# A hybrid decoder layer: the depthwise convolution wholly on VectorE, and the counting of a threshold search divided anew between ScalarE and VectorE

## The reference, cut to what matters

```python
s = einsum('thd,ld->thl', qi, ki) * 64 ** -0.5               # indexer
score = einsum('th,thl->tl', wi * 8 ** -0.5, relu(s))        # causal, -inf above the diagonal
_, idx = top_k(score, 256)                                   # 256 keys per query
attn = softmax(q . k[idx] + rel_bias) . v[idx]               # 8 heads x 64
u = glu_a * sigmoid(glu_b)                                   # 512 channels
conv = silu(layer_norm(depthwise_causal_conv(u, dw_w) + dw_b))   # 31 taps
y = x + concat(attn * silu(gate_a), conv * silu(gate_c)) @ w_out
```

## Time and profile before

| | us |
|---|---|
| runs | 1110.79, 1114.1, 1116.92 |
| the profiled execution | 1112.72 |
| its span | 1110.9 |
| PE busy | 965.8 (87%) |
| DVE busy | 762.6 (69%) |
| ACT busy | 388.1 (35%) |
| POOL busy | 178.4 (16%) |
| PE, DVE in the chain that ended last | 52%, 36% |

### The profile page before, as it was taken

The page is one execution under the profiler, slowest core; times in us unless marked ns, Lnnn a source line. Parts: engine busy times, 40 slices in busy tenths (PEclk is TensorE's granted clock), DMA queues, the critical chain, the costliest instruction groups (busy, mean ns, idle before and its releaser), DMA issues.

```text
span 1110.9 us, 11534 instructions
## 1 busy us (share of the span) xinstructions
PE 965.8 (87%) x3902; PEld 517.6 (47%) x3902; DVE 762.6 (69%) x1770; ACT 388.1 (35%) x808; POOL 178.4 (16%) x120
## 2 busy tenths in 40 slices
PE   3999999096899999999978999792899788899998
PEld 3866666063233444666433334441443433464443
DVE  5207979999897877999998889956777643552000
ACT  6311343141566545555510000216442432462000
POOL 0200699370342000000000000001013012000000
PEclk9899999588999999999998889896898997999999
DMA  7450020020472212020002000005024112100222
GB/s 276 149 183 0 1 76 2 0 77 0 152 231 81 105 38 96 1 76 1 1 9 104 20 19 11 1 0 198 21 84 116 30 39 57 29 2 12 76 76 66
DMA packets 35355, 69.89 MB, mean 63 GB/s; under 512 B 9633, under 2 KB 11977, under 8 KB 35289
## 3 DMA queue, kind: packets, MB, share of 16 engines
q1 hardware_dynamic: 28129, 43.99, 11.6%
q0 software_dynamic: 7168, 25.17, 7.1%
HBM read 58.50 MB, written 11.12 MB: 63 GB/s over the span
## 4 chain that ended last, share of the span: by engine, by line
PE 52%; DVE 36%; ACT 4%; issue 4%; DMA 2%; POOL 2%; SPq 0%; DVEq 0%; ACTq 0%; POOLq 0%
PE ps L485 48%; DVE ctmp L1297 11%; PE ps L488 4%; DVE junk L1363 4%; DVE eqm L1363 4%; POOL ctmp L1796 2%; DVE ct L1275 1%; ACT PTs L926 1%; DMA KVr<-in_cache_v,idx 1%; DVE Pm L1742 1%; DVE pv L1499 1%; DMA xn<-in_x_prompt 1%; DVE ps L1737 1%; DVE LG L1626 1%; DVE prod L1624 1%
## 5 line engine op out<-in xcount | busy, mean ns | idle before, releaser
L485 PE MATMUL ps<-xT,W 128*128 128x344 f32 x960 | 286.6, 461 | 1.8 <-ACT gcT L926 1.8
L485 PEld LDWEIGHTS ps<-xT,W 128*128 128x128 f32 x960 | 184.9, 194 | 101.5 <-issue 7.4
L485 PE MATMUL ps<-W,xT 128*128 128x512 f32 (+3 forms) x576 | 216.3, 534 | 2.0 <-ACT relu L1086 1.2
L1297 DVE SCALAR_TENSOR_TENSOR ctmp<-uT,chw,ctmp 128x1024 f32<-128x1024 f32 x90 | 172.4, 1916 | 3.1
L485 PEld LDWEIGHTS ps<-W,xT 128*128 128x128 f32 (+1 forms) x576 | 95.8, 187 | 115.3 <-issue 115.1
L1118 ACT ACTIVATE sgj<-SC,candn 128x1024 bf16<-128x1024 f32 (+2 forms) x96 | 88.6, 924 | 49.7 <-DVE candn L1379 49.7
L1796 POOL TENSOR_TENSOR ctmp<-ctmp,product 128x1024 f32<-128x1024 f32 x30 | 91.7, 3057 | 29.3 <-ACT product L1014 26.3
L1836 POOL DMA_INDIRECT KVr<-in_cache_k,idx x16 | 16.0, 999 | 469.9 <-DMA decode_q<-zN 386.3
L1719 DVE TENSOR_TENSOR resid<-resid,ps 128x512 f32<-128x512 f32 (+1 forms) x18 | 12.3, 686 | 86.8 <-PE ps L485 86.7
L926 ACT ACTIVATE PTs<-ps 128x512 f32<-128x512 f32 (+3 forms) x96 | 42.9, 481 | 80.9 <-PE ps L488 80.8
L1177 ACT ACTIVATE Pm<-Pm,mx 128x128 f32<-128x128 f32 (+7 forms) x64 | 49.5, 774 | 61.7 <-DVE mx L1745 60.4
(11 more groups left out here) (311 smaller groups left out, 1169.5 us busy)
## 6 DMA issues: line engine op xcount, KB each, us to landing
W<-in_w_in SPq DMA_DIRECT2D x8, 2048.0 KB, 8.8
xn<-in_x_prompt SPq DMA_DIRECT2D x8, 512.0 KB, 7.7
W<-in_w_out SPq DMA_DIRECT2D x1, 4096.0 KB, 16.0
resid<-in_x_prompt SPq DMA_DIRECT2D x16, 256.0 KB
out<-resid SPq DMA_DIRECT2D x16, 256.0 KB
out<-V SPq DMA_DIRECT2D x8, 256.0 KB
out<-zN SPq DMA_DIRECT2D x8, 256.0 KB
bias_rows<-tprow SPq DMA_DIRECT2D x1, 1536.0 KB, 9.4
```

The costliest lines, as they stand in the source:

```text
L485: return nc.tensor.matmul(out, lhsT, rhs, start=start, stop=stop)
L1297: ins = vec.scalar_tensor_tensor(acc_, src, chw[:, c, j:j + 1], acc_, ALU.mult, ALU.add)
```

## The change

All four chunks of the convolution become VectorE's: 124 taps in place of 93, with two slots of `ctmp` in turn. The last tap of a chunk writes into `conv` (the place in `uT`), after the chunk's `last_rows`. ScalarE's products and chunk copies and GpSimd's adds are gone, with their buffers and semaphores. The split of the taps in VectorE's order stays: 55 taps, `decode_u`, 57 taps, the block of small work, 12 taps.

In the search ScalarE counts blocks 7, 6, 4 and 2, VectorE 5 and 3 and the decode rows. `candn` is made straight from the threshold, ahead of `cand`; the bit of the round is a constant of the instruction and no longer a tile that is shifted; and the update is one predicated copy in place of a multiply and an OR. The order of the masks after the search follows the new order of the rows.

```diff
-    DVE_CHUNKS = [0, 2, 3]
-    POOL_CHUNK = 1
-    SLOT = {0: 0, 2: 1, 3: 0, 1: 2}
+    ACT_BLOCKS = (7, 6, 4, 2)
+    DVE_BLOCKS = (5, 3)
+    NA = len(ACT_BLOCKS)
+    DVE_CHUNKS = [0, 1, 2, 3]
...
             if n == 11:
-                wait(chunk_out, 4)
+                wait(taps_done, NTAP)
...
-        def chunk_copy(c):
...
-        def products(k):
...
-            for j, i in enumerate((7, 6, 2)):
+            for j, i in enumerate(ACT_BLOCKS):
...
-                if m == 2 * CW:
-                    v.wait_ge(chunk_out, 1)
                 src = uT[:, c, j:j + SEQ]
-                acc_ = ctmp[:, SLOT[c], :]
+                acc_ = ctmp[:, m // CW % 2, :]
...
                     v.wait_ge(taps_done, m)
-                    ins = vec.scalar_tensor_tensor(acc_, src, chw[:, c, j:j + 1], acc_, ALU.mult, ALU.add)
+                    if j == CW - 1:
+                        if c < 3:
+                            v.wait_ge(last_rows_read, c + 1)
+                        else:
+                            v.wait_ge(*plan.full("cp"))
+                    ins = vec.scalar_tensor_tensor(conv[:, c, :] if j == CW - 1 else acc_, src, chw[:, c, j:j + 1], acc_, ALU.mult, ALU.add)
...
-        rows = [sc(i) for i in (7, 6, 2, 5, 4, 3)] + [SD[:, :]]
+        rows = [sc(i) for i in ACT_BLOCKS + DVE_BLOCKS] + [SD[:, :]]
...
-            vec.tensor_scalar(candn[:, 0:3], cand[:, 0:3], 0x80000000, None, ALU.bitwise_xor).then_inc(cand_ready, 1)
-            count(ALU.is_ge, lambda j: cand[:, j:j + 1].bitcast(F32), 3)
+            count(ALU.is_ge, lambda j: cand[:, j:j + 1].bitcast(F32), NA)
...
+        vec.memset(candn[:, 0:NA], 0x80000000).then_inc(cand_ready, 1)
...
-            link(vec.tensor_tensor(cand[:, 0:7], thr[:, 0:7], bit[:, 0:7], ALU.bitwise_or))
+            bit = 1 << (BITS - 1 - r)
+            vec.tensor_scalar(candn[:, 0:NA], thr[:, 0:NA], bit, 0x80000000, ALU.bitwise_or, ALU.bitwise_xor).then_inc(cand_ready, 1)
+            link(vec.tensor_scalar(cand[:, 0:7], thr[:, 0:7], bit, None, ALU.bitwise_or))
             count_shared(r + 1)
             link(vec.scalar_tensor_tensor(tk[:, 0:7], cnt[:, 0:7], TOPK - 0.25, sgn[:, 0:7], ALU.is_ge, ALU.not_equal))
-            link(vec.tensor_tensor(tk[:, 0:7], tk[:, 0:7], bit[:, 0:7], ALU.mult))
-            link(vec.tensor_tensor(thr[:, 0:7], thr[:, 0:7], tk[:, 0:7], ALU.bitwise_or))
-            link(vec.tensor_scalar(bit[:, 0:7], bit[:, 0:7], 1, None, ALU.logical_shift_right))
+            link(vec.copy_predicated(thr[:, 0:7], tk[:, 0:7], cand[:, 0:7]))
...
-        def add_taps(k):
...
-        add_taps(CW)
         g.wait_ge(u_done, PIECES)
```

More of the change, by code:

```diff
@@ L185, in build @@
     ct = sb("ct", [P, 4, 1024], F32, rQK + 16384)
-    sgj = sb("sgj", [P, 3, SEQ], BF16, rQK)
+    sgj = sb("sgj", [P, 4, SEQ], BF16, rQK)
     qT = sb("qT", [P, 4, SEQ], F32, rQK)
@@ L204, in build @@
     kiS = sb("kiS", [NB, HD], F32, rGC + 16128)
-    ctmp = sb("ctmp", [P, 3, SEQ], F32, rGC)
+    ctmp = sb("ctmp", [P, 2, SEQ], F32, rGC)
     gcT = sb("gcT", [P, 4, SEQ], F32, rGC)
@@ L215, in build @@
     relu = sb("relu", [P, 2, 1024], F32, rV)
-    product = sb("product", [P, 2, SEQ], F32, rV)
     sc16 = [sb("sc16a", [16, 32, 2, 16], F32, rKV), sb("sc16b", [16, 32, 2, 16], F32, rV + 8192)]
@@ L300, in build @@
     candn = sb("candn", [P, 8], U32)
-    bit = sb("bit", [P, 8], U32)
     cnt = sb("cnt", [P, 8], F32)
-    acnt = sb("acnt", [P, 3], F32)
-    halfn = sb("halfn", [P, 3], F32)
+    acnt = sb("acnt", [P, 4], F32)
+    halfn = sb("halfn", [P, 4], F32)
     sgn = sb("sgn", [P, 8], F32)
@@ L389, in build @@
     ki_stored = sem("ki_stored")
-    product_ready = sem("product_ready")
-    product_added = sem("product_added")
     uzero_done = sem("uzero_done")
@@ L396, in build @@
     taps_done = sem("taps_done")
-    chunk_out = sem("conv_chunk_out")
     chain_s = sem("dve_chain")
@@ L994, in piece_out @@
             copy(dst, pt(tag)[:, 0:n], tag, func=func)
-        tap_next = [0]
-        def products(k):
[L1000 to L1015, removed]
         for c in range(4):
@@ L1020, in _ @@
                 piece_out("glub", m, uT[:, c, CW - 1 + a:CW - 1 + a + n], sT[:, 0], ACT.Sigmoid)
-                if c >= 2:
-                    products(2)
             for m in range(3 * c, 3 * c + 3):
@@ L1027, in _ @@
                 piece_out("glua", m, glua_r[:, m % 2, 0:n], sT[:, 1], ACT.Copy)
-                if c >= 2:
-                    products(1)
-        chunk_copy(0)
         for j, m in enumerate(QI_PIECES):
@@ L1091, in _ @@
                 done += 1
-            if n == 3:
-                chunk_copy(3)
         def evacuate(g, m):
@@ L1241, in _ @@
         link(vec.memset(Qb[:].rearrange("p a b c d -> p (a b c d)"), 0.0))
-        for j, i in enumerate((7, 6, 2)):
+        for j, i in enumerate(ACT_BLOCKS):
             link(vec.memset(halfn[:, j:j + 1], (i + 1) * P / 2.0))
-        link(vec.memset(bit[:], 1 << 30))
         v.wait_ge(small_in, 16 * 6)
@@ L1377, in count_shared @@
         def count_shared(r):
-            vec.tensor_scalar(candn[:, 0:3], cand[:, 0:3], 0x80000000, None, ALU.bitwise_xor).then_inc(cand_ready, 1)
-            count(ALU.is_ge, lambda j: cand[:, j:j + 1].bitcast(F32), 3)
+            count(ALU.is_ge, lambda j: cand[:, j:j + 1].bitcast(F32), NA)
             v.wait_ge(act_counted, r + 1)
-            link(vec.scalar_tensor_tensor(cnt[:, 0:3], acnt[:, 0:3], 0.5, halfn[:, 0:3], ALU.mult, ALU.add))
+            link(vec.scalar_tensor_tensor(cnt[:, 0:NA], acnt[:, 0:NA], 0.5, halfn[:, 0:NA], ALU.mult, ALU.add))
         def add_units(dst, a, units_):
@@ L1786, in _ @@
         loaded(2)
-        added = [0]
-        def add_taps(k):
[L1791 to L1797, removed]
         for m in range(PIECES):
             a, n = piece_rows(m)
-            if m in (6, 9):
-                add_taps(6)
             g.wait_ge(*plan.drained(("zt", "glua", m)))
@@ L1806, in _ @@
             pool.tensor_tensor(d, d, glua_r[:, m % 2, 0:n], ALU.mult).then_inc(u_done, 1)
-            if m >= 6:
-                add_taps(1)
-        add_taps(CW)
         g.wait_ge(u_done, PIECES)
```

## The result

The changed kernel took 1084.08 us (four runs, 1082.98 to 1085.5) beside 1113.87 for the kernel before: a ratio of 0.9733, 95% interval 0.9704 to 0.9763. The forecast was 1088, in a range of 1077 to 1099. The profiled execution took 1085.5 us with a span of 1083.7; the span had been 1110.9, so 27.2 us are to be found in it.

A forecast was written before the change was run, and what follows sets the result against it. VectorE, slowed by GpSimd, bounds the convolution; coupled VectorE, ScalarE and TensorE the search. Gains 12.8 + 0.7 + 12.5 = 26.0 from 1112.72 give 1086.7, plus 1.4 for the median: 1088, range 1077 to 1099.

The forecast's parts named there:

- Convolution, 12.8 us: VectorE's taps, undisturbed by GpSimd, follow every 1.317 us; first score at 265.6 instead of 278.38 us: gain 12.8 us.
- the hole: VectorE idles before `decode_u` near 163 us, waiting for the last `glua` piece that ScalarE evacuates at 171.1: 8 us charged.
- The rival in which the taps stay slow: Convolution: if GpSimd isn't the cause, 120 taps keep their mean of 1.92 us: 1151 us in all, chance 0.06.
- The late `qi` pieces: TensorE's last two `qi` pieces behind `own_score` end by 265.5, beside the taps' end at 265.6: 0, 1 us either way.
- The rival with half clock for both pieces: Two late `qi` pieces on TensorE take 18.6 us instead of 11.15, ending 7 us after the taps: 1095, chance 0.10.
- `chunk_copy(3)`, 0.7 us: ScalarE loses this copy between the first score steps: 0.7 us gained, bounds 0 and 1.15.
- Search, 12.5 us: Faster search rounds, capped by TensorE's order up to `equal_before`: `chosen()` starts at 572.5 instead of 585.02, gain 12.5 us.
- The rival in which the search gives nothing: ScalarE counts four blocks in 4.7 us instead of 3.7, rounds stay as long as today: 1101 us, chance 0.07.
- rounds of `ga` and `gc` would be TensorE-paced at 4.65 us: Search: a round needs 4.6 us, not above TensorE's 4.65 per projection piece, so TensorE sets the pace.
- the cover in front of `chosen()`: TensorE's order covers 12 us of VectorE's, so VectorE, 20 us earlier, waits some 8 us there.
- The limit of 5.1 us per round: The search gain stays 12.5 us for any round up to 5.1 us.
- The rival with 8 us more: TensorE keeps its clock better in the `k` tiles behind `equal_before` and the index stage gains too: 1080 us, chance 0.07.

The follow-up runs named there:

- `pool_adds`: The changed kernel with 20 idle adds of 128x1024 on GpSimd behind the last GLU product, on tiles nobody else uses then: 1121.8 us.
- `longer_rounds`: The changed kernel with four idle small VectorE steps (4 x 0.2 us) more in each search round: 1096.46 us, ratio 0.9886 to the kernel before.
- `search_only`: The search of the changed kernel with the convolution of the kernel before: 1098.4 us, ratio 0.9882 to the kernel before.
- `equal_earlier`: The changed kernel with `equal_before` behind three `k` tiles instead of four: 1078.94 us, ratio 0.9713 to the kernel before.

## Why the prediction was right, step by step

*Convolution, 12.8 us.* Measured 12.7, and each part of it: the hole 8.11 (8 forecast), the block from `Qb` to the next tap 250.50 - 246.53 = 4.0, the first score right behind the last tap. That GpSimd was the cause rested on two tap lengths in the trace of before; the adds of `pool_adds`, and the products that cost nothing, show it. The rival in which the taps stay slow fell with them.

*The late `qi` pieces.* TensorE idled 25.43 us, and the two pieces took 12.42 us instead of 11.15. They stayed hidden, but not by much. From `own_score` to the end of the first relu it took 265.20 - 249.80 = 15.4 us, and the first score came 1.0 us after that. The prediction had no margin to show here, so that part was close to luck. The rival with half clock for both pieces (18.6) fell.

*`chunk_copy(3)`, 0.7 us.* Worth nothing: from the first score to `v` there are 91.90 us instead of 91.79. VectorE's wait of 0.97 us behind the copy is gone, but one instruction later it waits 0.66 us for TensorE, and 0.77 instead of 0.44 at a relu soon after. The term was worked out from two engines alternating, and the third sets the pace there; it lay just below its lower bound of 0. VectorE in the kernel before, then in the changed one:

```profile
281.93 0.62 DVE L1343 SCALAR_TENSOR_TENSOR SC<-relu,wI,SC 128x384 f32<-128x384 f32 x1 [0.97 <-ACT relu L1086]
...
270.19 4.62 DVE L1225 STREAM_TRANSPOSE ct<-cin 128x1024 f32<-128x1024 f32 x4 [0.66 <-PE ps L481]
```

*Search, 12.5 us.* Measured 13.9. TensorE's queue is the cap, as forecast, and VectorE waits 6.96 us in `chosen()` (8 forecast). The 1.4 us more are small: 111.15 instead of 111.6 for the pieces, 27.5 instead of 27.7 for the tiles, an `equal_before` of 0.28 instead of 0.59, to which TensorE now comes without a pause, and 0.04 instead of 0.3 from there to `chosen()`. The first of these is a slip: 441.79 to 446.42 is 4.63, not 4.65, and 24 x 4.63 = 111.1. The rival in which the search gives nothing fell: the Sign of 640 columns took 0.81 us, as interpolated.

*One step was wrong without a price:* that rounds of `ga` and `gc` would be TensorE-paced at 4.65 us. They are 4.58 us long, and ScalarE's four counts with VectorE's update behind them pace them. The waits of the changed kernel in 255 to 580 us (us in total, times, longest) show VectorE waiting for ScalarE in each round, ScalarE waiting for `candn` in 15 of them, and ScalarE waiting for TensorE's `v` tiles much more than for `gc` pieces:

```profile
DVE cnt L1335 <- ACT sgj L1069: 27.8, 32, 2.9
...
ACT V L922 <- PE ps L481: 20.6, 8, 2.7
...
ACT sgj L1069 <- DVE candn L1357: 6.2, 15, 0.6
...
ACT gcT L922 <- PE ps L481: 2.9, 8, 0.6
```

A piece takes TensorE 111.31 / 24 = 4.64 us, a round 4.58: ScalarE, which starts behind TensorE after the `v` stretch, gains 0.06 us per round and meets TensorE again only among the `gc` pieces. The step rested on a round estimated at 4.6 against a piece of 4.65, too close to call. The forecast did not hang on it, as the cover in front of `chosen()` took either. The timeline of the changed kernel has the Sign of 640 columns, and the predicated copy, which took 0.17 us like the OR that it replaced:

```profile
428.56 0.81 ACT L1069 ACTIVATE sgj<-SC,candn 128x640 bf16<-128x640 f32 x1
...
517.67 0.17 DVE L1361 COPY_PREDICATED thr<-tk,cand 128x7 uint32<-128x7 uint32 x1
```

*The limit of 5.1 us per round was too wide.* It counted 12 us of cover, up to the first scan, and left out `norm(0)` behind it; the prediction's own 8 us of waiting leave 4.65 + 8 / 21 = 5.03, and the measured wait 4.58 + 6.96 / 23 = 4.9 us. `longer_rounds`, with some 0.8 us more per round, lies beyond it and lost 11.3 us. (VectorE's own round was also mis-summed: 5.58 less 0.88 and twice 0.2 is 4.3, not 4.4. Neither enters the 12.5.)

*What was left out:* 1.3 us between `chosen()` and the end, within the 2 us allowed; the fifth `k` tile took 8.81 us where it had taken 9.57. The rival with 8 us more did not come. Over the whole span, terms that came out too high and too low nearly cancel: 27.2 us measured and 26.0 forecast agree better than their parts. The other 2.8 us between 1088 and 1084.08 are spread: the forecast put the median 1.4 us above the profiled execution, and this time the profiled execution was the slowest of four, 1.4 above the median.

## What to carry to other kernels

Before work is shared out to an idle GpSimd, look how long the same VectorE instruction takes with and without it: here GpSimd's adds spared VectorE 31 taps (31 x 1.317 = 41 us), and the other 90 were longer beside GpSimd's work by 172.4 - 90 x 1.285 = 57 us. With the wait of 6 us that went and the one of 8 that came, this makes some 14 us, where 12.7 were measured. A faster loop brings no more than the queue of the next engine lets through; read which instruction waits at the loop's end, what stands in front of it in its own engine's order, and move that instead. When work moves between engines, look for waits that were free because the waiting engine came late: this one cost 8 us, and letting seven more taps go ahead of it won 7 of them back.

## What the runs showed of the hardware

In the twelve profiles the attention, from its first matmuls to the end of the span, has one of two lengths. It begins on TensorE with a small group of four matmuls behind a wait of 2.5 us. In ten profiles that group took 0.49 us, and the rest of the span from there 354.8 to 356.6 us; in those of `search_only` and `equal_earlier` it took 0.80 us, and the rest 359.8 and 359.7 us. These two kernels have no edit in common that the others lack.

The longer first group is a sign and not the cost. The granted clock in the first 6 us is 0.65 to 0.73 in the ten and 0.50 in the two, but the next such group comes 6.3 us behind the first in the changed kernel (728.08 to 734.37) and in `equal_earlier` (723.23 to 729.53) alike, and GpSimd's gathers of cached rows stand at the same distances up to 91.7 us. The kinds part behind that: from 85 to 92 us after the first matmul the granted clock is 1.00 in all ten and 0.76 in both others, and a gather that comes at 107.6 us in the changed kernel comes at 110.7 in `equal_earlier`. The stretches of 7 us (changed kernel, `equal_earlier`, in the columns of the earlier trace rows):

```profile
813.08:820.08 7.00, 5.97 (x28) 2.50 (x28) 6.65 (x13) 0.81 (x2) 3.26 (x4) 1.00 0.27 75
...
808.23:815.23 7.00, 5.97 (x10) 1.72 (x8) 6.25 (x12) 0.81 (x2) 3.37 (x4) 0.76 0.28 81
```

So some 3 of the 4 us go with a lower granted clock there. What decides whether it falls, and whether this makes the spread of the runs, some 8 us for one kernel, was not tried.
